# Stores of the delta-rule mixer moved from SyncE's queue to ScalarE's, with an earlier clearing of S and an earlier scaling of q

## The chip, the core and the metric

The kernel runs on one core of a Trainium2 chip. The metric is the device time of one execution, in microseconds (us).

## What is computed

Two layers of a streaming encoder, for 1024 prompt frames and 32 sample frames which share the weights, all in float32. The part that matters here is mixer A of layer 0, a gated DeltaNet with 8 heads of 128 x 128, in chunks of 64 frames:

```python
u, a_raw, b_raw, z_a, ... = split(rms_norm(x) @ w_in)
u, new_buf = causal_conv(u, conv_buf, conv_w)        # width 4; new_buf: last 3 rows, an output
q, k, v = split(silu(u));  q = l2_norm(q) * dk ** -0.5;  k = l2_norm(k)
# per chunk (gdn_block), G = cumsum(g), dec = exp(G_i - G_j) for i >= j
a_mat = where(strict, beta * (k k^T) * dec, 0) + I
sol = triangular_solve(a_mat, [beta v, beta exp(G) k])
u = sol_v - sol_k S
o = (q S) * exp(G) + (q k^T * dec) u
S = S * exp(g_last) + k^T (exp(g_last - G) u)        # the last S is an output
o = rms_norm(o) * silu(z_a)
```

The outputs of this mixer are `o`, the last three conv inputs of prompt and sample, and the final state S of both.

## The kernel before

The program goes in blocks: memory keys and values, norm, `gdn` (this mixer, about 175 to 1040 us), `band`, output projection, memory attention, then the second layer. Each block has its own instruction list for each engine, ordered by hand, and semaphores between them.

`gdn` loops over 8 heads. The first and the last are written out, heads 1 to 6 are a hardware loop. All 1056 frames of a head lie in 9 tiles of 128, handled in 3 groups of 3 tiles. While head h is computed, TensorE also projects the inputs of head h + 1: 12 jobs (z, v, k, q by three column ranges) of 8 steps (two instructions each). `fill(n)` puts n of these steps at fixed places between the stages of head h (`FILL`: 8 steps at "turn", 4 at "k", 4 at "q", and so on); what is left over runs at the head's end. The last head has no such fill.

The stages of a head are:

- VectorE copies the head's parameters and then waits for ScalarE's last copy of the projection (`proj_out`). It copies the tails (L1328), and computes the width-4 convolution of k and of q (L1335, L1338), each followed by a SiLU on ScalarE (L1196, L1197). Between the two it finishes the last third of the previous head's output. The convolution of v runs on GpSimd one head ahead.
- TensorE transposes k (L1038), forms k k^T (L1046), transposes q (L1056), forms q k^T (L1063), and transposes v and the tails (L1073, L1076).
- The triangular solve goes through 6 levels. At each, GpSimd multiplies AT by a mask into BT (L1526, three groups), TensorE multiplies BT by TM (L1083), ScalarE copies, TensorE multiplies by TT (L1094), and VectorE subtracts and transposes. At level 0 GpSimd first makes KE, at level 3 it scales q by EG = exp(G) into WQ (L1511), at levels 4 and 5 it makes KZ. ScalarE makes EG (L1233) after the squares of q.
- The chain over 17 chunks: for each, TensorE multiplies WQ by S (L1128), VectorE forms Ub (L1419), TensorE multiplies KZ by Ub (L1134), VectorE updates S (L1428). VectorE clears S (L1395) just before the chain, after a wait for the previous head's state store (`st_p`).

SyncE (SP) issues every DMA of the block from one queue in this order for head h: the four weight loads of head h + 1 (L934, each as soon as TensorE is done with that slot), the state stores of head h - 1 (L942, L943), its output stores (L956, L957), the gate rows of head h + 1 (L937), the six tail stores of head h (L950, L951).

Of the kernel before, what the change touches and what calls it, by code (L numbers as in the profile page):

```python
# [8 lines left out]
ALU = mybir.AluOpType  # L9
AX = mybir.AxisListType  # L10
ds = bass.ds
# [17 lines left out]
def wait(eng, sem, value):  # L29

    if not isinstance(value, int) or value > 0:
        eng.wait_ge(sem, value)
# [759 lines left out]
H_A = 8  # L792
# [19 lines left out]
def gdn(nc, ident, ones, eps, hT, W, w_ld, w_in, conv_w, conv_state, a_log, dt_bias, onorm_g, state_in,  # L812
# [4 lines left out]
    with ExitStack() as ctx:  # L817
# [81 lines left out]
        def steps_at(place, n=0):  # L899

            at = 0
            for name in ("turn", "k", "q", "qk", "v"):
                at += FILL[name]
                if name == place:
                    return at
            if place == "level":
                return at + FILL["level"] * n
            at += FILL["level"] * LAST + FILL["chain"]
            return at + (FILL["ws"] + FILL["su"]) * n

        def g3(buf, g):
            return buf[:, 3 * g:3 * g + 3, :]
# [4 lines left out]
        def by_token(col, g):  # L917
            return col[:, 3 * g:3 * g + 3].unsqueeze(2).broadcast_to([128, 3, 128])
# [11 lines left out]
        with nc.Block() as block:  # L930
            @block.sync
            def _(sp):
                def load_w(n, j, col):
                    sp.dma_start(W[:, j, :, :], w_cols[:, :, ds(col, 128)]).then_inc(w_ld[j], 16)  # L934

                def load_gates(n):
                    sp.dma_start(GB[:, 0:CW], gate_rows[0, ds(n, 1), 0:CW].to_broadcast([128, CW])).then_inc(gb_ld, 16)  # L937

                def store_state(h):

                    sp.wait_ge(s_ok, h * N + N)
                    sp.dma_start(state_p[ds(h, 1), :, :].rearrange("o d v -> d (o v)"), S[:, 0, :]).then_inc(st_p, 16)  # L942
                    sp.dma_start(state_s[ds(h, 1), :, :].rearrange("o d v -> d (o v)"), Sn[:, :]).then_inc(st_s, 16)  # L943

                def store_tails(h):

                    sp.wait_ge(tail_out, h + 1)
                    for j in (1, 2, 0):
                        col = h * 128 + 1024 * j
                        sp.dma_start(conv_p[:, ds(col, 128)], tailsT[3 * j:3 * j + 3, :]).then_inc(st_tail, 16)  # L950
                        sp.dma_start(conv_s[:, ds(col, 128)], tailsT[9 + 3 * j:12 + 3 * j, :]).then_inc(st_tail, 16)  # L951

                def store_out(h):

                    sp.wait_ge(o_fin, h * 3 + 3)
                    sp.dma_start(o_dram[ds(h * 128, 128), 0:NP], OF[:, 0:NP]).then_inc(st_o, 16)  # L956
                    sp.dma_start(o_dram[ds(h * 128, 128), NP:NTOK], OF[:, NP:NTOK]).then_inc(st_o, 16)  # L957

                def head(h, before):

                    for p, j in enumerate(ORDER):

                        sp.wait_ge(proj_done, h * 12 + 3 * p + 3)
                        load_w(h + 1, j, h * 128 + 128 + COL[j])
                    if before:
                        store_state(h - 1)
                        store_out(h - 1)
                    sp.wait_ge(eg_ok, h + 1)
                    sp.wait_ge(diffs, h * TILES + TILES)
                    load_gates(h + 1)  # L970
                    store_tails(h)

                sp.wait_ge(padded, 2)
                load_gates(0)
                head(0, False)
                with sp.Fori(1, H_A - 1) as h:
                    head(h, True)
                sp.wait_ge(proj_done, H_A * 12)
                load_ahead(sp, ahead)
                store_state(H_A - 2)  # L980
                store_out(H_A - 2)
                store_tails(H_A - 1)
                store_state(H_A - 1)
                store_out(H_A - 1)
                sp.wait_ge(st_tail, H_A * 96)
                sp.wait_ge(st_p, H_A * 16)
                sp.wait_ge(st_s, H_A * 16)
                sp.wait_ge(st_o, H_A * 32)

            @block.tensor  # L990
            def _(pe):
# [165 lines left out]
            def _(act):  # L1157
# [22 lines left out]
                def gates(n, g):  # L1180

                    act.wait_ge(diffs, n * TILES + 3 * g + 3)
                    act.activation(g3(dec, g), g3(dec, g), ACT.Exp).then_inc(dec_ok, 1)

                def head(h, more, before):
                    left = list(range(12)) if more else []

                    def jobs(steps):

                        while left and 8 * (left[0] + 1) <= steps:  # L1190
                            proj_copy(h + 1, left.pop(0))
# [39 lines left out]
                    act.activation(rk[:, :], rk[:, :], ACT.Exp, scale=0.5).then_inc(rk_ok, 1)  # L1231
                    act.wait_ge(gb_ld, h * 16 + 16)
                    act.activation(EG[:, :], GB[:, :], ACT.Exp).then_inc(eg_ok, 1)  # L1233
                    jobs(steps_at("v"))
                    act.wait_ge(q_sq, h * 3 + 3)
                    for l in range(1, LEVELS):
# [38 lines left out]
                        gates(h + 1, 2)  # L1275
                    jobs(96)

                for m in range(12):
                    proj_copy(0, m)
                act.preload_act_table_set("natural_log_exp_and_others")  # L1280
# [3 lines left out]
                with act.Fori(1, H_A - 1) as h:  # L1284
                    head(h, True, True)
                head(H_A - 1, False, True)

            @block.vector
            def _(dve):
# [23 lines left out]
                def head(h, more, before):  # L1313
# [8 lines left out]
                    dve.wait_ge(params, h * 5 + 1)  # L1322
                    wait(dve, conv_step, h * 8)
                    dve.tensor_copy(U[:, 0:2, NP + 3:NP + 6], cwc[:, 0:2, 4:7]).then_inc(params, 1)
                    wait(dve, v_turn, h * 4)
                    dve.wait_ge(proj_out, h * 12 + 12)
                    tv = tails[:, :].rearrange("p (k j r) -> p k j r", k=2, j=3)
# [63 lines left out]
                    for g in range(3):  # L1391
                        dve.wait_ge(u0_done, h * 3 + g + 1)
                        dve.tensor_tensor(g3(CU, g), p3(X3, g), by_token(cc, g), ALU.mult).then_inc(cu_ok, 1)
                    wait(dve, st_p, h * 16)
                    dve.memset(S[:, 0, :], 0.0).then_inc(s_zero, 1)  # L1395
                    if more:
                        next_gates(h + 1)

# [57 lines left out]
            def _(pool):  # L1456
# [36 lines left out]
                def head(h, more, before):  # L1493
                    wait(pool, ws_done, h * N)
                    wait(pool, s_ok, h * N)
                    pool.tensor_copy(Ss[:, :], sall[:, ds(h, 1), :].rearrange("p o n -> p (o n)")).then_inc(ss_ok, 1)
                    if before:
                        scale_out(h - 1, 2)
                    pool.wait_ge(params, h * 5 + 4)
                    wait(pool, w_done, h * 3)  # L1500
                    wait(pool, su_done, h * N)
                    for l in range(LEVELS):
                        if l == 0:
                            for g in range(3):
                                pool.wait_ge(k_rows, h * 3 + g + 1)
                                pool.tensor_tensor(g3(KE, g), g3(KR, g), by_token(cur[:, 1, :], g), ALU.mult).then_inc(ke_ok, 1)
                        elif l == 3:
                            pool.wait_ge(eg_ok, h + 1)
                            pool.wait_ge(silu, h * 6 + 4)
                            for g in range(3):  # L1510
                                pool.tensor_tensor(WQ[:, 3 * g:3 * g + 3, 1:3, :].rearrange("p t s n -> p t (s n)"),  # L1511
                                                   act3[:, 0, 384 * g:384 * g + 384].rearrange("p (t n) -> p t n", t=3),
                                                   EG[:, 384 * g:384 * g + 384].rearrange("p (t n) -> p t n", t=3),
                                                   ALU.mult).then_inc(qg_ok, 1)
                        elif l >= 4:
                            a = l - 4
                            for g in range(3):
                                pool.tensor_tensor(g3(KZ[:, a, :, :], g), g3(KR, g), by_token(cz[:, a, :], g), ALU.mult).then_inc(kz_ok, 1)
                        mask = level[:, l, :].unsqueeze(1).broadcast_to([128, 3, 128])
                        for g in range(3):  # L1520
                            pool.wait_ge(at_ok, h * 3 + g + 1)
                            if l == 1:
                                pool.wait_ge(tt_ok, h * 18 + g + 1)
                            elif l > 1:
                                pool.wait_ge(v_done, h * 15 + 3 * (l - 2) + g + 1)
                            pool.tensor_tensor(g3(BT, g), g3(AT, g), mask, ALU.mult).then_inc(masked, 1)  # L1526
                    if more:
                        taps_v(h + 1)
                        conv_values(h + 1, range(3))
                    scale_out(h, 0)  # L1530
                    if more:
                        conv_values(h + 1, range(3, 7))
                    scale_out(h, 1)
# [1178 lines left out]
```

## Time and profile before

| | |
|---|---|
| time, median of 3 runs | 3901.07 us (3896.49 to 3902.14) |
| profiled execution | 3896.49 us, of which the span (first to last instruction) 3894.8 us |
| mean granted TensorE clock | 0.964 |
| busy: TensorE matmul, VectorE, ScalarE, GpSimd | 93%, 29%, 28%, 12% |

PE is the matmul side of TensorE and PEld its weight loads, DVE is VectorE, ACT ScalarE, POOL GpSimd, SP SyncE; SPq and ACTq are the sequencers that issue DMAs. Idle time in square brackets is that of the engine just before the row, with what ended it. Times of a timeline count from the start of the span.

### The profile page before, as it was taken

The numbers are of one execution on the slowest core, as the hardware profiler recorded it, in microseconds if no ns is written. First come the engines' busy times: TensorE is split into PE (matmuls) and PEld (weight loads), VectorE is DVE, ScalarE is ACT, GpSimd is POOL, SyncE is SP. The second block draws the span as 40 slices with busy tenths as digits, with TensorE's granted clock in tenths as the row PEclk, the third lists the DMA queues.
The fourth block names the chain that finished last, engine by engine and source line by source line (L and its number), as shares of the span: only waits on it lengthen the run. The fifth ranks groups of instructions, "written<-read, shape, count | busy, mean of one in ns | idle before, by whom it ended". The sixth has DMA issues, their size and how long they took to land. (4 is left out here: it accounts for less than half of the span.)

```text
span 3894.8 us, 46760 instructions
## 1 busy us (share of the span) xinstructions
PE 3631.9 (93%) x16220; PEld 2509.8 (64%) x16220; DVE 1118.3 (29%) x2751; ACT 1104.3 (28%) x2773; POOL 466.8 (12%) x473
## 2 busy tenths in 40 slices
PE   6799999998799999999899988999999999699988
PEld 3377777776577777777544564677777777444564
DVE  1235555555323333333200023012222211201022
ACT  1333333333233333333201133022222222201140
POOL 0044444444100000000000000000000000000000
PEclk9799999999799999999999999999999999799999
DMA  5112231112022232211323004111111110423003
GB/s 158 46 29 35 35 34 34 34 29 29 25 39 39 41 43 42 38 42 33 126 68 120 23 14 142 45 33 36 46 46 46 41 41 16 151 66 123 23 12 123
DMA packets 238329, 208.89 MB, mean 54 GB/s; under 512 B 24679, under 2 KB 211975, under 8 KB 238167
## 3 DMA queue, kind: packets, MB, share of 16 engines
q1 hardware_dynamic: 224606, 178.79, 19.2%
q10 hardware_dynamic: 13568, 28.07, 1.9%
q8 instruction: 92, 1.51, 0.2%
q14 instruction: 63, 0.52, 0.0%
HBM read 158.01 MB, written 48.82 MB: 53 GB/s over the span
## 5 line engine op out<-in xcount | busy, mean ns | idle before, releaser
L1001 PE MATMUL gdn_pj<-hT,Wb 128*128 128x352 f32 x1536 | 514.0, 461 | 2.9 <-DVE gdn_OI L1445 2.9
L2272 PE MATMUL gla_pj<-hT,Wb 128*128 128x352 f32 x1536 | 470.0, 460 | 2.2 <-PEq L2132 1.6
L1739 PE MATMUL band_pj<-hT,Wb 128*128 128x384 f32 (+1 forms) x1152 | 386.6, 465 | 13.0 <-DVE band_tick L2060 10.0
L2272 PEld LDWEIGHTS gla_pj<-hT,Wb 128*128 128x128 f32 x1536 | 290.5, 190 | 151.2 <-issue 2.9
L563 PE MATMUL out_Y<-out_W,out_oS 128*128 128x512 f32 (+1 forms) x864 | 373.7, 592 | 0.0
L1001 PEld LDWEIGHTS gdn_pj<-hT,Wb 128*128 128x128 f32 x1536 | 266.2, 192 | 91.8 <-DVE gdn_OI L1445 3.0
L563 PEld LDWEIGHTS out_Y<-out_W,out_oS 128*128 128x128 f32 (+1 forms) x864 | 156.7, 181 | 214.1 <-issue 214.1
L1739 PEld LDWEIGHTS band_pj<-hT,Wb 128*128 128x128 f32 x1152 | 207.3, 193 | 94.9 <-DVE band_tick L2060 10.4
L2268 PE MATMUL gla_pj<-gla_Wv,hT 128*128 128x256 f32 x1152 | 264.9, 380 | 0.0
L289 PE MATMUL mem_pj<-hT,finish_Wq 128*128 128x352 f32 x768 | 235.3, 466 | 3.0 <-PEq L45 3.0
L2268 PEld LDWEIGHTS gla_pj<-gla_Wv,hT 128*128 128x128 f32 x1152 | 217.6, 190 | 29.6
L289 PEld LDWEIGHTS mem_pj<-hT,finish_Wq 128*128 128x128 f32 x768 | 148.3, 193 | 85.9 <-issue 6.7
L597 ACT ACTIVATE out_sqr<-out_xS 128x1024 f32<-128x1024 f32 (+1 forms) x18 | 19.0, 1056 | 495.3 <-DVE out_xS L624 495.3
L563 PE MATMUL out_Y<-Wb,out_oS 128*128 128x512 f32 (+1 forms) x288 | 131.4, 611 | 22.5 <-DMA out_oS<-o_features 22.5
L624 DVE TENSOR_TENSOR out_xS<-out_xS,out_Y 128x1024 f32<-128x1024 f32 (+1 forms) x18 | 21.9, 1219 | 450.9 <-PE out_Y L563 450.9
L1526 POOL TENSOR_TENSOR gdn_BT<-gdn_AT,gdn_level 128x384 f32<-128x384 f32 x144 | 144.0, 1029 | 31.9 <-DVE gdn_TT L1369 15.4
L1769 PE MATMUL band_pj<-Wb,hT 128*128 128x128 f32 x1152 | 144.2, 276 | 0.0
L563 PE MATMUL mo_Y<-finish_Wo,mo_oS 128*128 128x512 f32 (+1 forms) x288 | 130.0, 611 | 12.2 <-DMA mo_oS<-om_features 12.2
L1922 ACT ACTIVATE band_E<-band_NS,band_nm 128x576 f32<-128x576 f32 (+9 forms) x136 | 89.6, 659 | 181.1 <-DVE band_nm L1999 163.7
L1830 PEld LDWEIGHTS band_PX<-band_ET,band_VT 128*128 128x128 f32 x976 | 127.2, 192 | 19.4 <-issue 1.2
L1769 PEld LDWEIGHTS band_pj<-Wb,hT 128*128 128x128 f32 x1152 | 136.5, 192 | 0.7
L379 POOL COPY mem_Q<-mem_QN 128x512 f32<-128x512 f32 (+2 forms) x18 | 10.3, 577 | 1040.8 <-POOLq L260 980.6
(382 smaller groups left out, 4997.2 us busy)
## 6 DMA issues: line engine op xcount, KB each, us to landing
Wb<-in_l_w_in_dram SPq DMA_DIRECT2D x96, 512.0 KB, 7.9
out_oS<-o_features SPq DMA_DIRECT2D x16, 1024.0 KB, 5.8
out_W<-in_l_w_out_dram SPq DMA_DIRECT2D x6, 2048.0 KB, 15.3
o_features<-gla_OF ACTq DMA_DIRECT2D x16, 528.0 KB, 5.5
mkv_W<-in_l_w_mkv_dram SPq DMA_DIRECT2D x2, 4096.0 KB, 25.3
x_prompt<-out_xS ACTq DMA_DIRECT2D x16, 512.0 KB, 5.5
finish_Wq<-in_l_w_mq_dram SPq DMA_DIRECT2D x8, 1024.0 KB, 8.6
mo_xS<-x_prompt SPq DMA_DIRECT2D x16, 512.0 KB, 3.4
```

Source lines behind the costliest of these rows:

```text
L289: mm = pe.matmul(pj[:, m % 2, 0:w], W[:, k, 128 * j:128 * j + 128], hT[:, k, c0:c0 + w], start=k == 0, stop=k == KD - 1)
L563: mm = pe.matmul(Y[p][0:r, c:c + 512], oS[p][:, k, 0:r], W[:, k % per, c:c + 512], start=k == 0, stop=k == kt - 1)
L597: act.activation(sqr[0:r, :], xS[p][0:r, :], ACT.Square, accum_out=ss[0:r, p, 0:1]).then_inc(ssq, 1)
L624: dve.tensor_tensor(xS[p][0:r, :], xS[p][0:r, :], Y[p][0:r, :], ALU.add).then_inc(x_new, 1)
L1001: mm = pe.matmul(pj[:, m % 2, 0:w], W[:, j, k, :], hT[:, k, c0:c0 + w], start=k == 0, stop=k == KD - 1)
L1526: pool.tensor_tensor(g3(BT, g), g3(AT, g), mask, ALU.mult).then_inc(masked, 1)
L1739: mm = pe.matmul(out[:, 0:w], W[:, j, k, :], hT[:, k, c0:c0 + w], start=k == 0, stop=k == KD - 1)
L1769: mm = pe.matmul(out[:, 0:128], hT[:, k, 128 * i:128 * i + 128], W[:, 3, k, :], start=k == 0, stop=k == KD - 1)
L1830: mm = pe.matmul(PX[:, 1, :], v, ET[:, u % 2, 128 * b:128 * b + 128], start=b == 0, stop=b == blocks(u) - 1)
L1922: act.activation(E[:, u % 2, a:a + keys(u)], NS_[:, u % 2, 0:keys(u)], ACT.Exp, scale=-1.0, bias=nm[:, u:u + 1], accum_out=rsum[:, u:u + 1 ...
L2268: mm = pe.matmul(pj[:, m % 2, 0:DV_C], hT[:, k, 128 * x:128 * x + 128], Wv[:, k, :], start=k == 0, stop=k == KD - 1)
L2272: mm = pe.matmul(pj[:, m % 2, 0:w], W[:, SLOT[kind], k, :], hT[:, k, c0:c0 + w], start=k == 0, stop=k == KD - 1)
```

## The change

1. All stores of the block are issued by ScalarE (ACT) in place of SP. SP keeps the weight loads and the gate rows, in one loop.
2. At the end of a head, after its last projection copy, ScalarE issues the six tail stores and then the two state stores. The output stores of head h - 1 follow the making of EG in head h.
3. VectorE clears `S[:, 0, :]` at the start of a head, with the wait for the previous head's state store, ahead of the wait for the projection and of the tail copies.
4. GpSimd scales q by EG at level 1, ahead of that level's masks, not at level 3.

```diff
@@ sync
-                    if before:
-                        store_state(h - 1)
-                        store_out(h - 1)
                     sp.wait_ge(eg_ok, h + 1)
                     sp.wait_ge(diffs, h * TILES + TILES)
                     load_gates(h + 1)
-                    store_tails(h)
...
@@ scalar
+                def store_head(h):
+                    act.wait_ge(o_fin, h * 3 + 3)
+                    act.dma_start(o_dram[ds(h * 128, 128), 0:NP], OF[:, 0:NP]).then_inc(st_o, 16)
+                    act.dma_start(o_dram[ds(h * 128, 128), NP:NTOK], OF[:, NP:NTOK]).then_inc(st_o, 16)
...
                     act.activation(EG[:, :], GB[:, :], ACT.Exp).then_inc(eg_ok, 1)
+                    if before:
+                        store_head(h - 1)
                     jobs(steps_at("v"))
...
                     jobs(96)
+                    hd = h if isinstance(h, int) else act.snap(h)
+                    act.wait_ge(tail_out, h + 1)
+                    for j in range(3):
+                        col = h * 128 + 1024 * j
+                        act.dma_start(conv_p[:, ds(col, 128)], tailsT[3 * j:3 * j + 3, :]).then_inc(st_tail, 16)
+                        act.dma_start(conv_s[:, ds(col, 128)], tailsT[9 + 3 * j:12 + 3 * j, :]).then_inc(st_tail, 16)
+                    act.wait_ge(s_ok, h * N + N)
+                    act.dma_start(state_p[ds(h, 1), :, :].rearrange("o d v -> d (o v)"), S[:, 0, :]).then_inc(st_p, 16)
+                    act.dma_start(state_s[ds(h, 1), :, :].rearrange("o d v -> d (o v)"), Sn[:, :]).then_inc(st_s, 16)
...
@@ vector
                     dve.tensor_copy(U[:, 0:2, NP + 3:NP + 6], cwc[:, 0:2, 4:7]).then_inc(params, 1)
+                    wait(dve, st_p, h * 16)
+                    dve.memset(S[:, 0, :], 0.0).then_inc(s_zero, 1)
                     wait(dve, v_turn, h * 4)
                     dve.wait_ge(proj_out, h * 12 + 12)
...
-                    wait(dve, st_p, h * 16)
-                    dve.memset(S[:, 0, :], 0.0).then_inc(s_zero, 1)
@@ gpsimd
-                        if l == 0:
+                        if l < 2:
                             for g in range(3):
-                                pool.wait_ge(k_rows, h * 3 + g + 1)
-                                pool.tensor_tensor(g3(KE, g), ..., ALU.mult).then_inc(ke_ok, 1)
-                        elif l == 3:
-                            pool.wait_ge(eg_ok, h + 1)
-                            pool.wait_ge(silu, h * 6 + 4)
-                            for g in range(3):
-                                pool.tensor_tensor(WQ[...], act3[...], EG[...], ALU.mult).then_inc(qg_ok, 1)
+                                if l == 0:
+                                    pool.wait_ge(k_rows, h * 3 + g + 1)
+                                    pool.tensor_tensor(g3(KE, g), ..., ALU.mult).then_inc(ke_ok, 1)
+                                else:
+                                    if g == 0:
+                                        pool.wait_ge(eg_ok, h + 1)
+                                        pool.wait_ge(silu, h * 6 + 4)
+                                    pool.tensor_tensor(WQ[...], act3[...], EG[...], ALU.mult).then_inc(qg_ok, 1)
```

## Rows read from the trace of the kernel before

**Rows 1.** The page's head: busy us, share of the span, instructions

```profile
PE 3631.9 (93%) x16220; PEld 2509.8 (64%) x16220; DVE 1118.3 (29%) x2751; ACT 1104.3 (28%) x2773; POOL 466.8 (12%) x473
```

**Rows 2.** All waits of TensorE's matmuls, 400 to 900 us: total, times, longest

```profile
PE gdn_P L1083 <- DVE gdn_TM L1372: 2.4, 5, 0.5
PE gdn_X L1056 <- ACT gdn_act L1197: 2.0, 5, 0.4
```

**Rows 3.** VectorE's timeline, the clearing of S in two heads: start, duration

```profile
490.43 0.17 DVE L1395 MEMSET gdn_S<- 128x128 f32 x1
...
591.38 0.17 DVE L1395 MEMSET gdn_S<- 128x128 f32 x1
```

**Rows 4.** VectorE's timeline at a head boundary

```profile
536.57 0.17 DVE L1328 COPY gdn_tails<-gdn_U 128x9 f32<-128x9 f32 x1 [2.19 <-ACT gdn_U L1176]
```

**Rows 5.** ScalarE's timeline, 529 to 600 us

```profile
536.35 0.19 ACT L1176 ACTIVATE gdn_U<-gdn_pj 128x32 f32<-128x32 f32 x1
...
542.71 0.24 ACT L1197 ACTIVATE gdn_act<-gdn_conv 128x64 f32<-128x64 f32 x1
...
554.55 1.15 ACT L1233 ACTIVATE gdn_EG<-gdn_GB 128x1152 f32<-128x1152 f32 x1
558.46 0.49 ACT L1241 ACTIVATE gdn_VV<-gdn_P 128x384 f32<-128x384 f32 x1 [2.75 <-PE gdn_P L1083]
```

**Rows 6.** TensorE's timeline, 529 to 565 us

```profile
543.25 1.15 PE L1038 MATMUL gdn_X<-ident,gdn_act 128*128 128x128 f32 x9
...
549.15 1.20 PE L1056 MATMUL gdn_X<-ident,gdn_act 128*128 128x128 f32 x9 [0.39 <-ACT gdn_act L1197]
...
557.48 2.34 PE L1083 MATMUL gdn_P<-gdn_TM,gdn_BT 128*128 128x128 f32 x18 [0.48 <-DVE gdn_TM L1372]
```

**Rows 7.** SP's queue, 534 to 564 us: issues

```profile
536.14 0.37 SPq L934 DMA_DIRECT2D Wb<-in_l_w_in_dram  x1
536.81 0.37 SPq L942 DMA_DIRECT2D out_dram<-gdn_S  x1
...
560.07 0.27 SPq L950 DMA_DIRECT2D out_dram<-gdn_tailsT  x1
...
561.98 0.24 SPq L951 DMA_DIRECT2D out_dram<-gdn_tailsT  x1
```

**Rows 8.** Landing of L942's stores, of L2455's, and of a weight load at 637.09

```profile
DMA to landing us min/median/max: 1.5/8.6/15.4
...
DMA to landing us min/median/max: 1.7/3.7/4.9
...
Wb<-in_l_w_in_dram SPq DMA_DIRECT2D x1, 512.0 KB, 8.9
```

**Rows 9.** TensorE's timeline at gaps; stretches: busy by engine, granted clock, DMA

```profile
948.15 2.18 PE L1038 MATMUL gdn_X<-ident,gdn_act 128*128 128x128 f32 x9 [8.07 <-ACT gdn_act L1197]
...
1430.93 0.47 PE L1810 MATMUL band_PT<-ident,band_E 128*128 128x128 f32 x1 [2.73 <-DVE band_E L2017]
...
2358.27 15.89 PE L563 MATMUL mo_Y<-finish_Wo,mo_oS 128*128 128x512 f32 x32 [6.24 <-DMA mo_oS<-om_features]
...
948.20:952.40 4.20, 4.20 (x20) 4.20 (x21) 2.59 (x2) 4.10 (x21) 1.63 (x2) 0.50 0.75 62
2358.30:2362.10 3.80, 3.80 (x5) 1.73 (x6) 0.00 (x0) 0.00 (x0) 0.00 (x0) 0.50 0.84 312
1426.00:1436.00 10.00, 7.27 (x23) 4.15 (x22) 0.92 (x6) 0.11 (x2) 0.00 (x0) 0.83 0.73 56
```

**Rows 10.** GpSimd's timeline, 525 to 600 us

```profile
555.28 6.36 POOL L1526 TENSOR_TENSOR gdn_BT<-gdn_AT,gdn_level 128x384 f32<-128x384 f32 x6 [1.85 <-DVE gdn_TT L1369]
561.59 2.92 POOL L1511 TENSOR_TENSOR gdn_WQ<-gdn_act,gdn_EG 128x384 f32<-128x384 f32 x3
```

**Rows 11.** Timelines at the end of the block: ScalarE, SP's queue

```profile
1034.47 0.21 ACT L1273 ACTIVATE gdn_rs<-gdn_rs 128x3 f32<-128x3 f32 x1
...
1037.12 0.33 SPq L956 DMA_DIRECT2D o_features<-gdn_OF  x1
```

More of the change, by code:

```diff
@@ L937, in load_gates @@
                     sp.dma_start(GB[:, 0:CW], gate_rows[0, ds(n, 1), 0:CW].to_broadcast([128, CW])).then_inc(gb_ld, 16)
[L939 to L959, printed above, removed]
+                sp.wait_ge(padded, 2)
+                load_gates(0)
+                with sp.Fori(0, H_A - 1) as h:
                     for p, j in enumerate(ORDER):
@@ L970, in head @@
                     load_gates(h + 1)
-                    store_tails(h)
[L973 to L977, printed above, removed]
                 sp.wait_ge(proj_done, H_A * 12)
                 load_ahead(sp, ahead)
[L980 to L988, printed above, removed]
             @block.tensor
@@ L1286, in _ @@
                 head(H_A - 1, False, True)
+                store_head(H_A - 1)
+                act.wait_ge(st_tail, H_A * 96)
+                act.wait_ge(st_p, H_A * 16)
+                act.wait_ge(st_s, H_A * 16)
+                act.wait_ge(st_o, H_A * 32)
             @block.vector
@@ L1502, in head @@
                     for l in range(LEVELS):
-                        if l == 0:
+                        if l < 2:
                             for g in range(3):
-                                pool.wait_ge(k_rows, h * 3 + g + 1)
-                                pool.tensor_tensor(g3(KE, g), g3(KR, g), by_token(cur[:, 1, :], g), ALU.mult).then_inc(ke_ok, 1)
-                        elif l == 3:
-                            pool.wait_ge(eg_ok, h + 1)
-                            pool.wait_ge(silu, h * 6 + 4)
-                            for g in range(3):
[L1511 to L1514, printed above, removed]
+                                if l == 0:
+                                    pool.wait_ge(k_rows, h * 3 + g + 1)
+                                    pool.tensor_tensor(g3(KE, g), g3(KR, g), by_token(cur[:, 1, :], g), ALU.mult).then_inc(ke_ok, 1)
+                                else:
+                                    if g == 0:
+                                        pool.wait_ge(eg_ok, h + 1)
+                                        pool.wait_ge(silu, h * 6 + 4)
+                                    pool.tensor_tensor(WQ[:, 3 * g:3 * g + 3, 1:3, :].rearrange("p t s n -> p t (s n)"),
+                                                       act3[:, 0, 384 * g:384 * g + 384].rearrange("p (t n) -> p t n", t=3),
+                                                       EG[:, 384 * g:384 * g + 384].rearrange("p (t n) -> p t n", t=3),
+                                                       ALU.mult).then_inc(qg_ok, 1)
                         elif l >= 4:
```

## The prediction

> **What bounds the kernel now.** I read the page's head first: TensorE is busy 93% of the span, no other engine over 29% [rows 1]. So a change is worth what it does to TensorE's queue. I then asked what TensorE waited for in the middle heads (400 to 900 us): two rows, 4.4 us in 500 [rows 2]. There is nearly nothing to win there, and whatever makes TensorE wait is lost in full, because its fill work is a fixed list of projection steps in program order. The head period is 591.38 - 490.43 = 100.95 us, both ends read at the clearing of S [rows 3].
>
> The slack around the edited places comes from the timelines of one head boundary (530 to 560 us). VectorE waits for ScalarE's last projection copy, copies the tails at 536.57 and begins the convolution of k [rows 4]. ScalarE's SiLU of k ends at 542.71 + 0.24 = 542.95 [rows 5], and TensorE, done with its fill, starts the k transposes at 543.25 [rows 6]: 0.3 us of slack. At the next meeting, the q transposes at 549.15, it already sits idle 0.39 us for the SiLU of q: no slack. In the level solve it waits 0.48 us at 557.48 for a transposed tile.
>
> **The change, part by part.**
>
> *The state store and the clearing of S.* Before, VectorE cleared S long after the store (issued 536.81 [rows 7], cleared 591.38 [rows 3], no idle). Now VectorE must see the previous head's store landed before it copies the tails, and ScalarE issues that store only after its last projection copy, behind six tail stores. The issue time: ScalarE's copy starts at 536.35 [rows 5] and its sequencer can go on from about 536.4. The six tail stores, the first and last of which stand here, go out from 560.07 to 561.98 on SP's queue [rows 7], so with one more spacing 2.3 us. The state store would be issued at about 538.8.
>
> How long it takes to land is the unknown. In this mixer it takes 1.5 to 15.4 us, median 8.6, but there it stands in one queue behind a 512 KB weight load; in the later mixer the same kind of store, with 256 columns for 128, issued by ScalarE beside a weight load on SP's queue, takes 1.7 to 4.9, median 3.7 [rows 8]. That is the nearest row and I take 3.7: landing at 542.5. The bounds are 1.5 below; above, the weight load's own end, 536.14 + 8.9 = 545.0 [rows 7, 8], as the store shares engines with it. The clear is 0.17 us [rows 3], about 0.1 of it before the next instruction starts, so the tails start at 542.7 instead of 536.57: 6.1 us later (3.9 to 8.6). Queued behind the wait on VectorE are both convolutions, the last third of the previous head's output, and all that follows; ScalarE's SiLUs wait for these, and TensorE for the SiLUs. Its fill is used up at 543.25, so the lag arrives whole by the q transposes. There are seven boundaries with such a wait (none before the first head): 7 x 6.1 = 43 us.
>
> The Trainium skill, DMA: Bandwidth & Descriptors, section Queues, rings and completion order, says that each DMA engine takes turns between the queues it has work for. This would let the store pass most of the weight load, as the rows of the later mixer show. Its completion semaphore, says the same section, still comes after every earlier write of that engine on any queue. Held up so until the weight load is through, the store would land at 545.0 and the boundaries would cost 7 x 8.6 = 60 us in place of 43.
>
> *TensorE's clock.* The boundary becomes a gap of some 6 us. Gaps of that kind exist: 8.07 and 6.24 us, and after each TensorE ran on at the lower level, granted 0.50 (1.2 GHz), for 4.2 and 3.8 us [rows 9]. Half of 4.0 us is 2.0 us lost per boundary; less the 0.39 idle before the q transposes that it covers, 1.6 us. For six boundaries 10 us; the seventh has its gap and its slow stretch already. The bounds are 0 and 2.1 each.
>
> *The scaling of q on GpSimd (L1511) goes from level 3 to level 1.* At level 3 it was free: no wait there is in the list [rows 2]. At level 1 the masks start at 555.28, right after the first TT, and feed a TensorE that is waiting [rows 6, 10]. Now GpSimd first waits for EG, which ends at 554.55 + 1.15 = 555.70 [rows 5], then does three products, 2.92 us [rows 10], to 558.65, and then the three masks of 0.97 each: 559.6, 560.6, 561.6. TensorE started its three groups at 557.48 and takes 2.34 / 3 = 0.78 for each, so the third began at 559.0; now it begins at 561.6. The shift is 2.6 us. Later levels return nothing, since TensorE doesn't wait there. Eight heads: 21 us. The lower bound per head is 2.1 (559.6 - 557.48, if the later groups catch up), the upper 2.6 + 1.7 = 4.3: after a gap of 2.73 us elsewhere, 0.83 was granted over 10 us, so (1 - 0.83) x 10 = 1.7 us of full clock were missing [rows 9].
>
> *The freed queue.* SP loses ten stores a head. TensorE never waits for a weight load there [rows 2], so this is worth nothing. *The issues on ScalarE.* Two output stores of about 0.4 us behind EG fall in its 2.75 us of idle before 558.46 [rows 5]; the eight at the head's end lie inside VectorE's new wait; without that cover they would cost 3 us a head. *The clear taken out ahead of the chain.* In the middle heads TensorE has fill there; in the last, without fill, it is worth the clear's 0.17 us [rows 3]. *The end.* ScalarE's last exponential is at 1034.47; six tail and two state stores take 2.3 + 2 x 0.4 = 3.1 us, so the output store goes out at 1037.8 rather than 1037.12 [rows 11]: 0.7 us.
>
> Sum: 43 + 10 + 21 + 1 = 75 us on the profiled execution's 3896.5 (span 3894.8), which is the lowest of three runs with median 3901.1; 3896.5 + 75 = 3971.5 and 3901.1 + 75 = 3976. I take 3975.
>
> **The rivals.**
>
> *The store lands late.* Landings as on SP, 8.6 us, or at the weight load's end, add 2.5 to 4.9 us to each boundary: 3975 + 7 x (2.5 to 4.9) = 3993 to 4009. For it: S, tails and weights share the DMA engines, and the stores on SP's queue took 8.6 us [rows 8]. Against: the later mixer's stores [rows 8].
>
> *Only one of the two stalls is real.* If EG and the masks move apart so that the solve is fed in time (say the store's lag lets GpSimd run ahead), 21 us go: 3954. If the store lands in 1.5 us, 7 x 2.2 = 15 us go: 3960. Both together give 3939.
>
> *Not slower.* The price of both edits falls to nothing if TensorE isn't the one that meets the late engines: this needs fill for 6.1 us at the boundary, where the row shows 0.3. It decides at a landing before 536.57, ahead of the issue itself, or at tails which go to another place in the queue. Then only 0.17 us of gain and 0.7 at the end are left: 3902. I find no row for it but the missing wait at 543.25.
>
> *The clock stays down.* The Trainium skill, TensorE: Matmul & The Clock Gate, section HAM oscillation, tells of kernels where a gap in each round keeps throwing the clock back. This case's rows agree in kind: 8.07 us of idle, then 0.50 [rows 9]. What it would do here by the rows: each head has two gaps, 6 and 2.6 us; if the level solve too runs at 1.2 GHz, about 10 us of it, another 5 us for each of seven heads: 3975 + 35 = 4010.
>
> **How the numbers follow.** My case (3961 to 3992) 0.57; late landing 0.13; one stall gone or quick landing 0.17; clock down 0.08; not slower 0.05. The range 3942 to 4012 leaves out the last and the far ends. A change under 0.2% (8 us) is not told from none here: slower 0.95, same 0.03, faster 0.02.
>
> **What would show it.** Right: the clear (now ahead of the tail copies) idle about 6 us before each of seven, ended by the DMA of S; TensorE idle 5 to 7 us before the k transposes (L1038 before) in all heads but the first; its clock at 0.50 just after; the period 10 to 11 us longer; the level 1 masks on GpSimd 3 us later after TT and TensorE idle 2.5 to 3 us before them. Wrong: landing far from 3.7 us, no idle at the k transposes, the stall before level 1 under 1 us, or a granted clock of 1.00 through the gap.

## The result, and the profile after

The changed kernel takes 4017.7 us (median of 4 runs, 4013.6 to 4023.2) against 3901.1: ratio 1.030, interval 1.0285 to 1.032. It is slower by 117 us where 75 were forecast, and outside the range of 3942 to 4012. The direction and the places were right; the largest term was too small. Of the experiments below, one execution of e3 took 6653.6 us at a mean granted clock of 0.62 and is left out of that kernel's times.

The page's head: TensorE does the same instructions, with 28 us more busy time (its mean granted clock is 0.952 for 0.964) and 2 points less share [rows 1].

```profile
span 4013.2 us, 46771 instructions
PE 3659.7 (91%) x16220; PEld 2534.5 (63%) x16220; DVE 1117.3 (28%) x2751; ACT 1107.0 (28%) x2773; POOL 466.2 (12%) x473
```

The waits of TensorE's matmuls in the mixer, 174 to 1160 us (in us: total, times, longest). Line numbers have moved: L1001 is now the k transposes, L1019 the q transposes, L1046 the levels' first product. These answer to [rows 2].

```profile
PE gdn_X L1001 <- ACT gdn_act L1166: 86.1, 7, 33.0
PE gdn_P L1046 <- POOL gdn_BT L1513: 24.5, 8, 4.6
PE gdn_X L1019 <- ACT gdn_act L1166: 0.5, 1, 0.5
```

Both forecast stalls are there: 86 us at the k transposes, at seven boundaries, of which only 8.1 was there before (in the last head), and 24.5 before the level 1 product, where 5.6 was. The same stretch of the kernel before (174 to 1160 us):

```profile
PE gdn_X L1038 <- ACT gdn_act L1197: 8.1, 1, 8.1
PE gdn_P L1083 <- DVE gdn_TM L1372: 5.6, 8, 2.1
```

One middle boundary, first ScalarE's queue and then VectorE, answers to [rows 4, 7]:

```profile
454.22 0.28 ACTq L1253 DMA_DIRECT2D out_dram<-gdn_tailsT  x1
...
455.36 1.97 ACTq L1254 DMA_DIRECT2D out_dram<-gdn_tailsT  x1
...
458.24 0.36 ACTq L1256 DMA_DIRECT2D out_dram<-gdn_S  x1
```

```profile
463.39 0.17 DVE L1312 MEMSET gdn_S<- 128x128 f32 x1 [10.94 <-DMA out_dram<-gdn_S]
...
1057.48 0.17 DVE L1312 MEMSET gdn_S<- 128x128 f32 x1 [27.20 <-DMA out_dram<-gdn_S]
```

The fourth tail issue takes 1.97 us, not 0.25. So S goes out 4.0 us after the first tail store (2.3 forecast) and lands 5.1 us later (3.7 forecast). SP had issued the 512 KB weight load at 454.22, the same moment as the first tail store. The DMA issues there with the time to landing, the load and the state store:

```profile
Wb<-in_l_w_in_dram SPq DMA_DIRECT2D x1, 512.0 KB, 8.9
...
out_dram<-gdn_S ACTq DMA_DIRECT2D x1, 64.0 KB, 5.1
```

The load landed at 454.22 + 8.87 = 463.09 and the store at 458.24 + 5.07 = 463.31. It is so at all six middle boundaries: the store goes out 3.0 to 5.1 us after the load and lands 0.2 to 0.7 us after the load has, which takes 5.8 to 13.4 us. At the third, with the slowest load, the two read:

```profile
Wb<-in_l_w_in_dram SPq DMA_DIRECT2D x1, 512.0 KB, 13.4
...
out_dram<-gdn_S ACTq DMA_DIRECT2D x1, 64.0 KB, 8.7
```

The second of VectorE's rows above is the last boundary: it waits 27.2 us. There ScalarE's queue and the landings of all eight stores (line L1256) read:

```profile
1032.07 0.27 ACTq L1253 DMA_DIRECT2D out_dram<-gdn_tailsT  x1
...
1039.16 1.91 ACTq L1256 DMA_DIRECT2D out_dram<-gdn_S  x1
```

```profile
DMA to landing us min/median/max: 1.6/5.2/18.2
```

S goes out 7.1 us after the first tail and lands 18.2 us after that, at 1057.39. SP issues four loads, 2 MB, for the next block from 1031.92 on. They landed at 1045.15, 1051.66, 1058.73 and 1061.03: the store came in 1.3 us ahead of the third and 3.6 us ahead of the fourth, whose issue (1037.08 to 1046.79) was still going on when S went out.

TensorE's timeline for the second head after such a boundary, with the last head's start; then GpSimd's. They answer to [rows 6, 10].

```profile
470.19 2.15 PE L1001 MATMUL gdn_X<-ident,gdn_act 128*128 128x128 f32 x9 [8.72 <-ACT gdn_act L1166]
...
477.18 1.15 PE L1019 MATMUL gdn_X<-ident,gdn_act 128*128 128x128 f32 x9
...
487.81 4.21 PE L1046 MATMUL gdn_P<-gdn_TM,gdn_BT 128*128 128x128 f32 x18 [2.83 <-POOL gdn_BT L1513]
...
1065.23 2.18 PE L1001 MATMUL gdn_X<-ident,gdn_act 128*128 128x128 f32 x9 [33.00 <-ACT gdn_act L1166]
```

```profile
483.31 3.42 POOL L1498 TENSOR_TENSOR gdn_WQ<-gdn_act,gdn_EG 128x384 f32<-128x384 f32 x3 [2.86 <-ACT gdn_EG L1202]
486.68 3.87 POOL L1513 TENSOR_TENSOR gdn_BT<-gdn_AT,gdn_level 128x384 f32<-128x384 f32 x4
```

The clock after each of the two gaps, and ten us after it has come back (stretches: busy by engine, granted clock, DMA), as in [rows 9]:

```profile
470.20:473.50 3.30, 3.30 (x16) 3.30 (x17) 3.23 (x3) 3.21 (x15) 0.78 (x1) 0.50 0.00 0
473.60:483.60 10.00, 10.00 (x60) 7.92 (x59) 7.07 (x20) 9.22 (x36) 5.88 (x7) 1.00 0.06 23
487.90:493.90 6.00, 6.00 (x25) 5.50 (x26) 0.00 (x0) 1.47 (x3) 4.64 (x5) 0.50 0.00 0
```

TensorE runs at 1.2 GHz from the start both times, also after the gap of only 2.8 us.

**Where the time is.** I cut each head at the starts of four TensorE groups: k transposes, q transposes, first level product, first chain product (470.19, 477.18, 487.81 and 525.06 for the head above; the next begins at 590.85), and summed each stage over the heads. Less the same sums of the kernel before (us, by the profiled executions; `six` and `last` are the stretches from the chain's start to the next k transposes, at the six middle boundaries and at the last):

```
kernel              six   last  k to q  q to level  level to chain  other    span
before            313.7   53.4    47.3        66.2           272.0           3894.8
changed           +53.6  +24.9    +9.2       +18.6           +12.2   -0.1    +118.4
e1_pool_only        0.0    0.0    +0.1       +19.9           +11.6  +10.9     +42.5
e2_stores_clear   +56.6  +25.2   +10.2        -0.3            -2.4   +0.7     +90.0
e3_late_clear      +4.5   +6.4    +0.4       +19.8           +10.4   +1.8     +43.3
e4_stores_only     +4.3   +6.8    +0.4         0.0            -0.3   +2.0     +13.2
e5_state_first    +33.5   +7.3    +8.8       +18.7           +10.8   +1.1     +80.2
e6_state_early     +0.6   +1.9    +0.1       +19.8            +9.8   +1.6     +33.8
e7_ahead_held     +54.0   +3.4   +10.0       +18.6           +11.1   -3.0     +94.1
e8_load_later     +21.2  +24.9    +5.6       +18.8           +10.4   +2.6     +83.5
e9_early_clear_sp +52.6  +28.5   +10.3        -0.4            -2.4   +5.0     +93.6
e10_level2        +55.9  +24.4    +8.9        -0.3            -1.8   +1.1     +88.2
e11_early_level3   +0.7   +1.6    +0.2         0.0            -0.8   +1.8      +3.5
e12_paired          0.0    0.0     0.0        -5.8            +8.4   +3.5      +6.1
```

The profiled execution of before is its fastest run (the medians beside the experiments were 3902 to 3903), so a span difference reads some 7 us high. Totals below are medians against medians.

### The profile page after: what moved, and what is told of

It is laid out like the page before. It is cut to its first block and busy times, and to the rows that moved or that the text cites. A ratio compares the mean times of both kernels' runs of the same rounds, so it can differ in the third digit from the quotient of the medians.

```text
span 4013.2 us, 46771 instructions
## 1 busy us (share of the span) xinstructions
PE 3659.7 (91%) x16220; PEld 2534.5 (63%) x16220; DVE 1117.3 (28%) x2751; ACT 1107.0 (28%) x2773; POOL 466.2 (12%) x473
## 3 DMA queue, kind: packets, MB, share of 16 engines
q1 hardware_dynamic: 219710, 173.34, 18.2%
## 5 line engine op out<-in xcount | busy, mean ns | idle before, releaser
L1817 PE MATMUL band_PX<-band_ET,band_VT 128*128 128x128 f32 x976 | 131.7, 276 | 0.9 <-issue 0.9
## 6 DMA issues: line engine op xcount, KB each, us to landing
out_W<-in_l_w_out_dram SPq DMA_DIRECT2D x6, 2048.0 KB, 15.4
```

The lines of the kernel that those rows point to most:

```text
L1817: mm = pe.matmul(PX[:, 1, :], v, ET[:, u % 2, 128 * b:128 * b + 128], start=b == 0, stop=b == blocks(u) - 1)
```

## The experiments

**The scaling alone (e1).** The kernel before, with the new GpSimd order.

```diff
-                        if l == 0:        # KE
...
-                        elif l == 3:      # WQ = q * EG
...
+                        if l < 2:         # l == 0: KE; l == 1: WQ = q * EG
```

> The kernel before with one part of the change: GpSimd scales q at level 1. Stall theory: each of the 8 heads loses 2.3 us of idle before the level 1 product and 0.4 in its pace, as in the changed kernel's heads, plus up to 1.7 of slower clock after the gap: +22 to +31 us. Rival (the gap at level 1 costs clock only when the boundary's gap has come just before): +22 and a granted clock of 1.00 in the heads. Rival (the part is hidden by itself and costs only together with the late stores): within 3 us of before.

Measured: 3937.6 against 3903.4, ratio 1.0087 (1.0071 to 1.0104), +34 us, above the 22 to 31 expected; the stages' own sum, 31.6, is at its upper end.

```profile
PE gdn_P L1083 <- POOL gdn_BT L1527: 25.4, 8, 4.6
```

The stall stands alone, and slows the clock alone: 0.50 was granted over 469.3 to 472.7, 0.6 us after TensorE had gone on, with no boundary gap before. Both rivals fall. In the two heads where no slow stretch followed, "level to chain" grew by 0.5 us only (34.92 against 34.42). Of the span's 42.5 us, 10.9 lie outside the stages; where they come from stays open, and the medians say 34.

**The stores and the clear alone (e2).** The changed kernel, scaling at level 3.

> The changed kernel with the scaling of q back at level 3. If the boundary wait is the main cost: the stretch from the chain to the next k transposes stays 78 us longer in sum over seven boundaries, the stretch from k to q transposes about 9 us longer by the clock, the rest as before: +85 to +92 us. If the two parts feed each other, less than the changed kernel's 118 less the first experiment's cost.

Measured: 3980.5 against 3903.4, ratio 1.0197 (1.018 to 1.0214), +77 us.

```profile
PE gdn_X L1001 <- ACT gdn_act L1166: 89.4, 7, 33.3
...
PE gdn_P L1046 <- DVE gdn_TM L1360: 5.6, 8, 2.1
```

The stages moved as expected (56.6 + 25.2 and 10.2 by the clock), and so did the span (+90.0). The medians' 77 is below the expected 85 to 92: the profiled execution of before is 7 us under its median, and that of e2, 3986.5, is the longest of four, 6 us over its own. 34 + 77 = 111 of the 117: the two parts add up, within what the runs can tell.

**The clear back at the chain (e3)**, stores still on ScalarE, scaling at level 1.

```diff
-                    wait(dve, st_p, h * 16)                           # before the tail copies
-                    dve.memset(S[:, 0, :], 0.0).then_inc(s_zero, 1)
...
+                    wait(dve, st_p, h * 16)                           # after CU, before the chain
+                    dve.memset(S[:, 0, :], 0.0).then_inc(s_zero, 1)
```

> The changed kernel with the wait for the state store and the clear of S put back ahead of the chain; stores stay on ScalarE. If the early wait on the store is the cost of the boundary: TensorE's idle before the k transposes is gone in the middle heads and 8 us in the last, and +22 to +31 us is left, as in the kernel with the scaling alone. If the ten DMA issues on ScalarE cost something by themselves (they delay its table load and SiLU), 2 to 4 us a boundary are left on top: +36 to +59.

Measured: 3939.8 (the middle one of 3939.3, 3939.8 and 3942.4) against 3903.4, +36 us; ratio 1.0097 (1.0077 to 1.0117). That is above the theory's 22 to 31 and at the lower edge of the rival's 36 to 59. The middle boundaries fall from +53.6 to +4.5: the early wait is the cost there. But TensorE still waits 18.3 us at the k transposes against 8.1 before, so something of ScalarE's is left, 4.5 us over six boundaries and 6.4 at the last, less than the rival's 2 to 4 us at each but the last:

```profile
PE gdn_X L1001 <- ACT gdn_act L1166: 18.3, 5, 14.5
```

**The stores alone (e4)**: clear late, scaling at level 3.

> Only the move of the stores to ScalarE's queue is left of the change; clear of S late, scaling at level 3. Theory: hidden, within 3 us of before, the tail and state issues (4 us) end before ScalarE's SiLU of k at +5.3 us after its last copy. Rival (ScalarE's issues are on the path): +2 to +4 us for each of 7 boundaries, +14 to +28.

Measured: 3907.5 against 3903.4, ratio 1.0008 (0.9998 to 1.0017). By the median, +4 us, it is not told from none, yet the stages show +4.3 and +6.8 us in the trace. The interval ends at +6.6 us, so the median doesn't bear out all 11; why stays open. ScalarE at the last boundary:

```profile
946.62 2.02 ACTq L1254 DMA_DIRECT2D out_dram<-gdn_tailsT  x1
...
952.32 1.78 ACTq L1256 DMA_DIRECT2D out_dram<-gdn_S  x1
954.19 3.39 ACTq L1257 DMA_DIRECT2D out_dram<-gdn_Sn  x1
957.79 1.28 ACT L1165 ACT_TABLE_LOAD   x1 [12.05 <-issue]
```

Eight issues hold ScalarE for 12 us while the 2 MB of loads are out, and its SiLU of k comes late. The forecast had these issues hidden. At the last boundary they aren't, and at the middle ones not quite (0.7 us each).

**State stores ahead of the tails (e5)**, otherwise the changed kernel.

```diff
+                    act.wait_ge(s_ok, h * N + N)
+                    act.dma_start(state_p..., S[:, 0, :]).then_inc(st_p, 16)
+                    act.dma_start(state_s..., Sn[:, :]).then_inc(st_s, 16)
                     act.wait_ge(tail_out, h + 1)
                     for j in range(3):                      # six tail stores, then no state stores
```

> The changed kernel, but ScalarE issues the two state stores ahead of the six tail stores. In the changed kernel S went out 4.0 us after the first tail issue and landed about 5.2 us later. Theory (the boundary is issue time plus landing): S goes out 4.0 us earlier, six boundaries give back 4 us each and the last one more, since S is then queued before the DMA rings are full: 24 to 40 us below the changed kernel's 4018, so 3978 to 3994. Rival (the store lands when the weight load issued at the same moment is through, whenever it was issued itself): within 8 us of 4018.

Measured: 3980.4 against 3902.2, ratio 1.0206 (1.0189 to 1.0223): 37 us below the changed kernel, as expected. VectorE's wait for the store in all heads, and the landing:

```profile
L1312 DVE MEMSET gdn_S<- 128x128 f32 x8 | 1.3, 165 | 55.7 <-DMA out_dram<-gdn_S 55.7
```

```profile
DMA to landing us min/median/max: 1.5/6.3/8.4
```

93.7 us of waiting fell to 55.7, and the boundaries gave back 17.6 of 24.9 us at the last and 20 at the six others. But not as 4 us each. At the first, S went out 0.13 us ahead of the weight load and landed in 1.7 us: 7.1 us came back. At the five others it went out at the same moment as the load, landed 5.2 to 8.4 us later, 0.8 to 5.3 ahead of the load, and gave back 1.2 to 5.4. Together with the changed kernel, where the store behind the load landed 0.2 to 0.7 us after it, this says that what counts is the place relative to the load, not the issue time by itself. The rival is out for a store issued with the load; for one behind it, it describes every row.

**State stores ahead of the last projection copies (e6).** The same three lines stand before `gates(h + 1, 2)` and `jobs(96)`.

> The changed kernel, but the state stores go out ahead of ScalarE's last projection copies, some 4 us before VectorE would go on. Theory: the store is landed by the time that VectorE reaches the tails or less than 2 us later, also at the last boundary, because it is ahead of the weight loads; what is left is the level 1 stall (31 to 36 us over before) and the issues on ScalarE: 3935 to 3950. Rival (landing takes 9 us or more after whatever stands in the rings): 3970 or more.

Measured: 3931.0 against 3902.2, ratio 1.0075 (1.0058 to 1.0092), +29 us: 4 us better than the lower end expected.

```profile
L1312 DVE MEMSET gdn_S<- 128x128 f32 x8 | 1.3, 165 | 1.7 <-DMA out_dram<-gdn_S 0.9
```

```profile
DMA to landing us min/median/max: 1.5/1.5/2.3
```

With no load out, the store lands in 1.5 us and VectorE's wait is gone. Nearly all that the boundaries had cost goes with it (+0.6 and +1.9 are left), and the slow clock behind them.

**The next block's loads held (e7).** SP waits for the store of the last boundary before it issues the four loads.

```diff
                 sp.wait_ge(proj_done, H_A * 12)
+                sp.wait_ge(st_p, (H_A - 1) * 16)
                 load_ahead(sp, ahead)
```

> The changed kernel, but SP holds the four loads for the next block (2 MB) until the state store of the last boundary has landed. Theory: the 27.2 us wait of VectorE at the last boundary falls to 6 us or less, as there is nothing beside the store, and the full rings that made ScalarE's issues slow are empty: 19 to 24 us below the changed kernel, 3994 to 3999; the six other boundaries stay. Rival (the last boundary is long because it has no fill work, not because of these loads): within 4 us of 4018.

Measured: 3995.6 against 3902.2, ratio 1.0243 (1.0226 to 1.026): 22 us below the changed kernel. The last boundary falls from +24.9 to +3.4, the others stay at +54.0. So the 27 us wait came from these 2 MB. That full rings are what makes the issues slow is not shown; the run shows that without the loads they aren't slow.

**The fourth weight load sent later (e8)**, after the gate rows.

```diff
-                    for p, j in enumerate(ORDER):
+                    for p, j in enumerate(ORDER[:3]):
...
                     load_gates(h + 1)
+                    sp.wait_ge(proj_done, h * 12 + 12)
+                    load_w(h + 1, ORDER[3], h * 128 + 128 + COL[ORDER[3]])
```

> The changed kernel, but the fourth weight load of a head goes out after the gate rows, some 20 us after the boundary, so that at the six middle boundaries the state store meets no weight load. Theory: the slow tail issue (1 to 2 us) goes and the store lands in about 2 us in place of 5.2, so each of the six boundaries gives back 4 to 5 us: 24 to 30 us below the changed kernel, 3988 to 3994. Rival (the landing is the store's own time, with or without the load): within 8 us of 4018.

Measured: 3982.6 against 3902.2, ratio 1.0208 (1.019 to 1.0225): 35 us below the changed kernel, more than the 24 to 30 expected: the six boundaries gave back 5.4 us each, and 3.6 us of slow clock went with them. One middle boundary, VectorE, and the landings:

```profile
451.29 0.17 DVE L1314 MEMSET gdn_S<- 128x128 f32 x1 [5.71 <-DMA out_dram<-gdn_S]
```

```profile
DMA to landing us min/median/max: 1.6/1.6/18.4
```

Without the load the store lands in 1.6 us and goes out 2.3 us after the first tail. 21.2 us are left over six boundaries, 3.5 each: nearly the 2.3 + 1.6 of issue and landing. The 18.4 is the last boundary, where this kernel changes nothing.

**Early clear with the stores on SP's queue (e9)**: the kernel before, with only the wait and the clear moved to the head's start.

> The kernel before, stores on SP's queue as they were, scaling at level 3; only the wait for the state store and the clear of S are moved to the head's start. It tells whether ScalarE's queue has a part in the loss. In the kernel before, S is issued 0.67 us after the fourth weight load and lands 8.4 to 13.3 us later, so VectorE's tails would start about 9 us late at six boundaries (54 us or somewhat more); at the last boundary S is issued at 954.77, behind 2 MB of loads, and lands up to 15.4 us later, 29 us late. With 9 us for the clock: +88 to +98 us, about as much as the stores on ScalarE's queue with the same clear (+77 in this measurement) or 10 to 20 more. Rival (the loss comes from ScalarE's issues): under +40.

Measured: 3991.9 against 3903.3, ratio 1.0227 (1.0212 to 1.0243), +88.5 us. The forecast, made from rows of the kernel before and the changed kernel's 9 us of clock, held. ScalarE's queue isn't the loss. With it the same early clear costs 77 by the medians (e2), but the seven boundaries are alike in the two traces, 52.6 + 28.5 here and 56.6 + 25.2 in e2, and so are the other stages. The second queue gained 3.3 us at the last boundary and lost 4.0 at the six; where the 11 us between the medians lie stays open. SP's issues at the last boundary, the four loads and then S, whose own issue took 6.56 us:

```profile
1002.29 14.73 SPq L59 DMA_DIRECT2D Wb<-in_l_w_in_dram  x4
1017.06 6.56 SPq L942 DMA_DIRECT2D out_dram<-gdn_S  x1
```

**The scaling at level 2 (e10)**, otherwise the changed kernel.

```diff
-                        if l < 2:
+                        if l in (0, 2):
```

> The changed kernel with the scaling of q at level 2 in place of level 1. By the trace before, GpSimd is done with the level 1 masks at 558.2 and EG at 555.7, so the three products end at 561.1 and the level 2 masks at 562.1, 563.0 and 564.0, about as TensorE comes to them (563.4, 564.2, 564.9). Theory: the stall is gone with the slow stretch after it, 25 to 34 us below the changed kernel: 3984 to 3993. Rival (GpSimd is short of time at any early level): less than 12 us below 4018.

Measured: 3985.4 against 3903.3, ratio 1.0214 (1.0198 to 1.0229): 32 us below the changed kernel, as expected. One level later, the stall and its slow stretches are gone.

**Both costs taken away (e11)**: e6 with the scaling at level 3.

> The changed kernel with its two costs taken away: state stores ahead of ScalarE's last projection copies, scaling back at level 3. The tails stay on ScalarE behind the last copy, the clear stays early. If nothing else in the change costs time: within 6 us of the kernel before, as the slow tail issues on ScalarE at the last boundary may keep 2 to 3 us. If there is a third cost: more than 8 us over before.

Measured: 3899.5 against 3903.3, ratio 0.9994 (0.9985 to 1.0003). As expected: there is no third cost, and no gain either.

**Paired transposes (e12)**, on the kernel before, to win the 0.48 us at level 1.

```diff
                         dve.tensor_tensor(g3(TT, g), eye, g3(BT, g), ALU.subtract).then_inc(tt_ok, 1)
-                    for g in range(3):
                         dve.wait_ge(tt_ok, h * 18 + g + 1)
                         dve.transpose(g3(TM, g), g3(TT, g)).then_inc(tm_ok, 1)
```

> The kernel before, but VectorE transposes each group of TT right after making it, so that the first tile that TensorE waits for at level 1 (0.48 us in seven heads, 2.13 in the last) is ready sooner. By the stalls, up to 5.5 us faster (0.14%), too little to be told from no change: ratio 0.9975 to 1.001.

Measured: 3907.1 against 3903.3, ratio 1.001 (1.0001 to 1.0019). That is at the upper edge of what was expected. "q to level" falls by 5.8 us as reckoned, but "level to chain" grows by 8.4.

```profile
PE gdn_P L1083 <- POOL gdn_BT L1525: 7.8, 17, 1.0
```

TensorE now comes to the masks of GpSimd, which takes 1 us for each of the six of levels 1 and 2, ahead of them. The wait has only changed its name, and has grown by 2.6 us. Nothing tried here is measurably faster than the kernel before.

## Why the prediction was wrong

*What bounds the kernel.* Right. There was no slack at the boundary or at level 1, and every late engine became TensorE's wait in full.

*The state store and the clear: 43 us forecast, 78.5 measured (53.6 + 24.9).* This is the step that failed. The wait was where the prediction had it, as e3, e6, e7 and e8 show; its size was wrong in two places: "I take 3.7" for the landing, and "7 x 6.1" for the count. Of some 36 us missing, 17 lie in the six middle boundaries (8.9 us each for 6.1) and 19 in the last (24.9 for 6.1).

- The landing. At the six middle boundaries the store landed 0.2 to 0.7 us after the weight load that had gone out before it. The prediction had this value, the load's own end, as its upper bound: 8.6 us a boundary, against 8.9 measured as a mean of 6.2 to 13.5. The 3.7 us came from the later mixer [rows 8], and there the trace of before differs in two ways. The store goes out at most 0.14 us from its load, not 3 to 5 us behind it, and the load itself lands in 4.4 to 5.1 us at the middle boundaries, not 5.8 to 13.4; the store came in 0.8 to 2.6 us ahead of it. The 8.9 us used for the bound is also the load of another boundary; the one at 536.14 took 13.75.
- The issue. "2.3 us" was read from tails that go out with no load under way [rows 7]. Beside the weight load the six take 3.0 to 5.1 us, without it 2.3 (e8). Behind a load this hardly mattered, as the load set the landing. Without one the two add up: 2.3 + 1.6 us, and 3.5 us a boundary are left in e8.
- The last boundary. "7 x 6.1" took seven like ones. At the last one SP sends 2 MB, not 512 KB, and the loss is 24.9, of which e7 gives back 21.5. The trace of before had the warning in the 15.4 of [rows 8], the landing of just this store behind those loads, and I took that for the price of a shared queue. The rounds of a loop that are written out, first and last, need their own row.

*The skill's rule.* The Trainium skill, DMA: Bandwidth & Descriptors, section Queues, rings and completion order, has each engine take turns between queues. The trace agrees that both queues move at once: from 459 to 461 us of the changed kernel SP's moved 196 packets and ScalarE's 187. That didn't make the small store early. At the middle boundaries it landed just after the load, as in the prediction's other sum, 60 us, whose share for six, 52, is near the 53.6. At the last it passed the fourth load and, by 1.3 us, the third, but still took 18.2 us against 1.5 with nothing out. Whether turns of unequal packets or the ordered semaphore write hold it wasn't tried. The store's move to a second queue was worth nothing at the boundaries with the early clear (81.1 us in e9, 81.8 in e2).

*The clock: 10 us forecast, about 18 measured.* 9.2 us after the boundaries, as reckoned. The rest is half of the slow stretches behind the level 1 gap, which I had only as a bound: "level to chain" grew by 12.2, and eight times the 0.43 us by which it grew in the head with no slow stretch there (34.85 against 34.42) is 3.4. So 8.8 is clock, by this estimate. e1 shows it without any boundary gap.

*The scaling of q: 21 us forecast, 22 measured (18.6 + 3.4).* Right, with its working: 2.83 us idle before the product, 0.48 before. e10 shows that it takes one level to hide it.

*The freed queue: nothing.* Right (e4, e11). *The issues on ScalarE: nothing.* Wrong in e4's trace, by 6.8 us at the last boundary and 4.3 over the six others; in the changed kernel VectorE's wait covers them. *The end and the clear: +1.* The part after the mixer's last chain start is 0.9 us shorter, so the 0.7 at the end was not seen.

*The rivals.* "The store lands late" was the nearest, 3993 to 4009, and still short, as it too took seven equal boundaries. What it says of the store is what happened at the six. "The clock stays down" is partly so. "One stall gone" and "not slower" are out. The measured terms, 78.5 + 18 + 22 = 118.5, are the stages of the table in another order, so that they give the span's 118.4 is no further proof.

## What to carry to other kernels

When a wait on a store moves ahead of an engine's main work, look first at which load starts before the store goes out, and take that load's own landing as the store's, from the row of this very place. With no load out, price it as issue plus landing. Here a store ahead of the loads and of the last projection copies cost 0.6 us over six boundaries and 1.9 at the last (e6); behind them it cost 53.6 and 24.9 of a tensor engine that had 0.3 us of slack. And a row from a similar place is near only if the order of the issues is the same there.

Read the first and the last round of a loop on their own rows. And count each new gap of the tensor engine twice: once as idle time, once for the slow clock after it.

## What the runs showed of the hardware

- A 64 KB store landed in 1.5 to 1.6 us with no load out (e8, six boundaries; e6, the same). Issued 0.7 to 5.1 us behind a 512 KB load, on the same queue or on another engine's, it landed 0.2 to 0.9 us after that load in all 60 cases (before, changed, e1 to e4, e7, e9, e10, e12). Issued at the same moment it landed 0.8 to 5.3 us ahead of it (e5).
- Behind 2 MB of loads from another engine's queue it took 18.2 us (changed), and landed before the last two of the four loads. On the loads' own queue it landed after all four, 14.4 us after its issue (e9).
- Issuing is slowed by what another queue has out: a tail store of 1.5 KB mostly took ScalarE 0.25 to 0.3 us alone (e8), up to 2.25 beside a 512 KB load on SP's queue (e5), and ScalarE was held 12 us by eight issues beside 2 MB (e4).
- A gap of 2.8 us in dense TensorE work was followed by 0.50 granted clock for 3 to 6 us in most heads (seven of eight in the changed kernel, six in e1), not in all.
